# PEER gather of expert rows: two of each eight dot products moved from VectorE to GpSimd and ScalarE, h read from PSUM

## The chip, the cores and the metric

The kernel runs on one core of a Trainium2 chip, in float32. The metric is the device time of one execution in microseconds (us), from the first to the last instruction.

## The reference, cut to what matters

256 tokens of width 2048 go through a gated-MLP layer, an attention layer and a mixer with convolution and mLSTM; the last part is a layer of product-key experts (PEER). The change touches only that one. For each token 8 heads pick 16 of 16384 experts, so 128 picks a token:

```
ue  = take(u, eid)                                  # 128 rows of 2048 floats for each token
act = gelu(einsum('thkd,td->thk', ue, xt))          # one dot product of 2048 for each pick
ve  = take(v, eid)
out = einsum('thk,thkd->td', gate * act, ve)
```

What the change rearranges is the einsum in the second line: 256 tokens times 128 picks, each a dot of a gathered row of `u` with the token's row of h.

## The kernel before, in words

The tokens are two tiles of 128, one token in each partition. A pick of a tile is then one gather: an indirect DMA that GpSimd issues (L560) brings 128 rows of 8 KB, one to each partition, 1 MB in all. There are 256 of them, 128 in each tile. They land in `ring`, eight slots of SBUF; slot s holds pick s of a batch of eight.

VectorE does three things in this stage (L1887 to L1903):

- `choose(n)` finds the experts of a group n (2 heads, 32 picks, four batches) with maxima, index searches and one-hot look-ups. Eight groups, four to a tile; the choice of group n+1 stands ahead of the dots of group n, so no choice stands between groups 6 and 7.
- `dot_rows(n)` (L1838) waits for each slot to land (`gathered`, L1823) and does one fused multiply and sum over 2048 elements (L1847), both operands in SBUF: `ring[:, s, :]` and `h[:, t, :]`. After eight of them it copies the eight dots to `wgt` (L1856) and stages the indices of the batch after the next (`stage`, L1817).
- In tile 1 it also builds, once a batch, the one-hot matrices of eight tokens of tile 0 (`one_hots`, L1827). TensorE multiplies them (`scatter`, L917), and ScalarE stores the products as `wT` (`store_w`, L1209).

GpSimd runs a loop of 16 gathers (L549). It waits for `idx_ready` at the start of a batch, and before each gather for `rows_used`, the count of dots done, so that the slot it overwrites is free. Between the gathers it has no other work.

ScalarE does the exponentials of the gates (L1192), the gelu of a tile's dots (L1198), the copies of transposed picks (L1204) and the stores of `wT`.

At the end of a tile `weights(t)` (L1859) waits for the gelu, multiplies by the gates and waits until TensorE has transposed the weights and ScalarE has copied them out of PSUM (units `wgtT0`, `wgtT1`; the keys go the same way earlier, as `pkT0`, `pkT1`). Then the one-hots of tile 1 follow alone, and after them the product with the dense three quarters of `v` and the gathered last quarter.

PSUM is two halves of 2048 floats a partition, A and B, handed from unit to unit in the order of the list `UNITS` (L83). In this stage half A takes `scores1` and then both halves take the small units of the picks; the scatter alternates between A and B.

Of the kernel before, what the change touches and what calls it, by code (L numbers as in the profile page):

```python
# [71 lines left out]
SCATTER = 8  # L72
# [70 lines left out]
def build(nc, x, norm_g, a_w_in, a_v_norm_g, a_w_s, a_b_s, a_w_out, b_w_in, b_w_out, final_g, ln_in_g_2, ln_in_b_2,  # L143
# [6 lines left out]
    with ctx:  # L150
# [180 lines left out]
        def sem(name):  # L331
            return ctx.enter_context(nc.semaphore(name))
# [161 lines left out]
        def _(pool):  # L494
# [54 lines left out]
            with pool.Fori(0, TILES * PICKS // BODY) as i:  # L549
                for n in range(BODY):  # L550
                    b, s = divmod(n, GATHER_SLOTS)
                    if s == 0:
                        pool.wait_ge(idx_ready[b], i + 1)
                    if s == GATHER_SLOTS // 2:

                        pool.wait_ge(products, CHUNKS)

                    pool.wait_ge(rows_used, i * BODY + (n + 1))
                    pool.nop(nofuse=True)
                    nc.gpsimd.indirect_dma_start(  # L560
                        out=ring[:, s, :], out_offset=None, in_=peer_u_2[0],
                        in_offset=bass.IndirectOffsetOnAxis(ap=idx[:, b, s:s + 1], axis=0),
                    ).then_inc(row_landed[s], 16)
# [22 lines left out]
        def _(pe):  # L586
# [322 lines left out]
            def turn_picks(unit, srcs):  # L909

                is_free(pe, unit)
                hf = halves(unit)
                for n, src in enumerate(srcs):
                    last = nc.tensor.transpose(ps[hf][:, 3, n * P:(n + 1) * P], src, ident[:, :])  # L914
                filled_by(last, unit)

            def scatter(t):  # L917

                with pe.Fori(0, P // SCATTER // 2) as i:
                    for s in range(2):  # L920
                        m = i * 2 + (t * (P // SCATTER) + s)
                        pe.wait_ge(onehot_done, m + 1)
                        pe.wait_ge(w_stored, m + 1)
                        for n in range(SCATTER):
                            last = mm(by_128[s][:, n, :], onehot_b[:, s, n, :], onehot_a[:, s, n, :], start=True, stop=True)  # L925
                        last.then_inc(scattered, 1)

            pe.sem_inc(scattered, 2)
            emptied("peer_q1")()
            for t in range(TILES):  # L930
                pe.wait_ge(keys_known, t + 1)
                turn_picks(f"pkT{t}", [pick_keys[:, t, half, :] for half in range(2)])
                pe.wait_ge(wgt_done, t + 1)
                turn_picks(f"wgtT{t}", [wgt[:, t * PICKS:(t + 1) * PICKS]])
                scatter(t)

            def multiply_v(c, s, first=False, last=False):
# [31 lines left out]
        def _(act):  # L969
# [221 lines left out]
            scores_out(1)()  # L1191
            def gate_exponent(n):  # L1192
                t, q = divmod(n, TILE_GROUPS)
                act.wait_ge(gate_sub, n + 1)
                cut = gate[:, t, q * GROUP_HEADS:(q + 1) * GROUP_HEADS, :]
                fn(cut, cut, ACT.Exp).then_inc(gate_exp, 1)  # L1196

            def pick_gelu(t):  # L1198

                act.wait_ge(idx_ready[1], (t + 1) * PICKS // (2 * GATHER_SLOTS) + 1)  # L1200
                cut = wgt[:, t * PICKS:(t + 1) * PICKS]
                fn(cut, cut, ACT.Gelu).then_inc(gelu_done, 1)

# [5 lines left out]
            def store_w(t, first, count):  # L1209

                with act.Fori(0, count // 2) as i:
                    for s in range(2):
                        m = i * 2 + (first + s)
                        act.wait_ge(scattered, m + (t * (P // SCATTER) + 3))
                        fn(wT[:, 1 - t, :, bass.ds(m * SCATTER, SCATTER)],  # L1215
                           by_128[s][:, 0:SCATTER, :].rearrange("p n a -> p a n"), ACT.Copy).then_inc(w_stored, 1)
# [49 lines left out]
        def _(dve):  # L1266
# [571 lines left out]
            def dot_rows(n, batches=0):  # L1838

                t, q = divmod(n, TILE_GROUPS)  # L1840
                first = n * GROUP_PICKS
                per = batches // (GROUP_PICKS // BODY)
                with dve.Fori(0, GROUP_PICKS // BODY) as i:
                    for b in range(2):
                        for s in range(GATHER_SLOTS):
                            gathered(i, first + b * GATHER_SLOTS, s)
                            v.tensor_tensor_reduce(out=ring[:, s, :], in0=ring[:, s, :], in1=h[:, t, :], scale=1.0,  # L1847
                                                   scalar=0.0, op0=ALU.mult, op1=ALU.add,
                                                   accum_out=dots[:, b, s:s + 1]).then_inc(rows_used, 1)
                            done = b * GATHER_SLOTS + s + 1  # L1850
                            if done * per % BODY == BODY // 2:
                                m = q * batches + done * per // BODY
                                one_hots(m % 2, i * per + m, i * (per * SCATTER) + m * SCATTER)

                        dve.wait_ge(rows_used, i * BODY + (first + (b + 2) * GATHER_SLOTS))
                        v.tensor_copy(wgt[:, bass.ds(i * BODY + (first + b * GATHER_SLOTS), GATHER_SLOTS)], dots[:, b, :])  # L1856
                        stage(b, i * BODY + (first + (b + 2) * GATHER_SLOTS))

            def weights(t):  # L1859

                dve.wait_ge(gelu_done, t + 1)
# [4 lines left out]
                is_emptied(dve, f"wgtT{t}")  # L1866

            dve.sem_inc(rows_used, GATHER_SLOTS)
# [125 lines left out]
```

## Time and profile before

| | us |
|---|---|
| median of 3 runs (3248.04 to 3255.05) | 3249.94 |
| span of the profiled execution | 3249.8 |
| first gather to last dot (1815.8 to 2576.0 in the span) | 760 |
| VectorE busy / ScalarE / GpSimd / TensorE, whole span | 2225 / 1095 / 825 / 2417 |
| granted TensorE clock, mean of the span | 0.872 |

All times are positions in the span of the profiled execution or durations in it. The stage of the change lies between 1815 and 2576 us. Before it the stream of dense weights runs; after it the one-hots of tile 1 (to 2632) and the product with `v` (to the end).

### The profile page before, as it was taken

Reading aid. Unit: us, or ns where it says so; the run is one execution under the profiler, and the core shown is the slowest. Engines: PE = TensorE matmul, PEld = TensorE weight load, DVE = VectorE, ACT = ScalarE, POOL = GpSimd, SP = SyncE. Lnnn points to the kernel's source line nnn. Section 1 sums busy time; section 2 is a strip of 40 time slices with the busy share of each in tenths; the row PEclk is TensorE's granted clock in tenths of the full one; section 3 lists DMA queues with packets and bytes.
Section 4 is the critical chain, followed back from the end, with each engine's and each line's share of the span. In section 5 each row is a group of like instructions: output and inputs, shape, how many; then the busy total and the mean of one; then the engine's idle time right before and its main releaser. Section 6 shows DMA issues by size and latency. Waiting matters only on the chain.

```text
span 3249.8 us, 32810 instructions
## 1 busy us (share of the span) xinstructions
PE 2416.7 (74%) x10945; PEld 1994.8 (61%) x10945; DVE 2225.1 (68%) x2822; ACT 1095.1 (34%) x1069; POOL 824.5 (25%) x548
## 2 busy tenths in 40 slices
PE   7999999999999998999998400001111389998996
PEld 6888888888888886888887400001111267777775
DVE  4456455555445556356656899999999987777777
ACT  4444444444445543344444100000000134343343
POOL 1000000000000000000000466676557435555553
PEclk8999999999999998899999755555555699999998
DMA  7666556556665454455564688898789548888886
GB/s 246 194 187 185 178 181 188 186 190 188 185 184 162 136 201 157 143 162 182 181 231 140 267 368 363 373 410 339 308 315 381 230 166 287 284 285 296 282 284 211
DMA packets 164690, 766.49 MB, mean 236 GB/s; under 512 B 20124, under 2 KB 20176, under 8 KB 130672
## 3 DMA queue, kind: packets, MB, share of 16 engines
q1 hardware_dynamic: 104800, 415.28, 39.9%
q0 software_dynamic: 59792, 349.90, 27.7%
q8 instruction: 62, 1.02, 0.1%
q14 instruction: 36, 0.29, 0.0%
HBM read 763.00 MB, written 2.10 MB: 235 GB/s over the span
## 4 chain that ended last, share of the span: by engine, by line
PE 54%; DVE 25%; DMA 11%; issue 6%; ACT 3%; DVEq 1%; SPq 0%; POOL 0%; POOLq 0%; ACTq 0%
PE half L600 49%; DVE ring L1847 14%; DMA v_raw<-in_peer_v 9%; DVE v_split L1928 3%; ACT v_split L1229 2%; DVE onehot_a L1834 2%; PE half L619 1%; DMA v_rows<-in_peer_v,idx 1%; DMA w_raw<-in_a_w_in 1%; DVE onehot_b L1830 1%; PE half L941 1%; PE half L796 1%; DVEq L1834 0%; PE half L668 0%; DVE left L1745 0%
## 5 line engine op out<-in xcount | busy, mean ns | idle before, releaser
L600 PE MATMUL half<-w_split,xT 128*128 128x512 f32 x7104 | 1639.4, 392 | 14.8 <-DVE xT L1296 12.2
L600 PEld LDWEIGHTS half<-w_split,xT 128*128 128x128 f32 x7104 | 1338.1, 189 | 294.4 <-issue 8.1
L1277 DVE TENSOR_TENSOR w_split<-w_raw,w_split 128x1024 fp32r<-128x1024 f32 x592 | 722.5, 1225 | 764.6 <-ACT w_split L981 763.8
L981 ACT ACTIVATE w_split<-w_raw 128x1024 fp32r<-128x1024 f32 x592 | 626.5, 1059 | 943.2 <-PE half L600 914.8
L560 POOL DMA_INDIRECT ring<-in_peer_u,idx x256 | 480.9, 1878 | 439.6 <-DVE dots L1847 186.2
L941 PE MATMUL half<-v_split,w_x 128*128 128x512 f32 x2304 | 548.6, 395 | 46.0 <-ACT v_split L1229 43.3
L1847 DVE CUSTOM_DVE_ANT_0 ring<-ring,h 128x2048 f32<-128x2048 f32 x256 | 570.0, 2285 | 5.0 <-issue 2.5
L941 PEld LDWEIGHTS half<-v_split,w_x 128*128 128x128 f32 x2304 | 428.6, 189 | 165.8 <-ACT v_split L1229 76.0
L574 POOL DMA_INDIRECT v_rows<-in_peer_v,idx x256 | 327.9, 1281 | 333.6 <-DVE v_odd L1911 209.2
L925 PE MATMUL half<-onehot_a,onehot_b 128*128 128x128 f32 x512 | 95.0, 362 | 334.8 <-DVE onehot_a L1834 334.8
L925 PEld LDWEIGHTS half<-onehot_a,onehot_b 128*128 128x128 f32 x512 | 87.9, 268 | 342.1 <-DVE onehot_a L1834 342.1
L1928 DVE TENSOR_TENSOR v_split<-v_raw,v_split 128x1536 fp32r<-128x1536 f32 x128 | 225.0, 1758 | 102.4 <-ACT v_split L1229 102.3
L1229 ACT ACTIVATE v_split<-v_raw 128x1536 fp32r<-128x1536 f32 x128 | 190.6, 1489 | 292.5 <-DMA v_raw<-in_peer_v 292.5
L498 POOL DMA_DIRECT2D row_a<-in_final_g x1 | 0.5, 531 | 1130.2 <-DVE ao L1503 1130.2
L1215 ACT ACTIVATE wT<-half 128x1024 f32 x32 | 32.8, 1024 | 395.6 <-PE half L925 395.6
L914 PE MATMUL half<-ident,wgt 128*128 128x128 f32 x2 | 0.9, 473 | 186.2 <-DVE wgt L1863 186.2
L914 PE MATMUL half<-ident,pick_keys 128*128 128x128 f32 x4 | 1.0, 353 | 184.1 <-DVE v_odd L1877 184.1
L1911 DVE SCALAR_TENSOR_TENSOR v_odd<-v_rows,wgt,v_odd 128x512 f32<-128x512 f32 x128 | 95.8, 748 | 36.2 <-DMA v_rows<-in_peer_v,idx 35.8
L914 PEld LDWEIGHTS half<-ident,wgt 128*128 128x128 f32 x2 | 0.4, 180 | 186.8 <-DVE wgt L1863 186.8
L914 PEld LDWEIGHTS half<-ident,pick_keys 128*128 128x128 f32 x4 | 0.6, 177 | 184.3 <-issue 184.3
L1911 DVE SCALAR_TENSOR_TENSOR h<-v_rows,wgt,h 128x512 f32<-128x512 f32 x128 | 95.4, 745 | 7.1 <-DMA v_rows<-in_peer_v,idx 7.1
L1196 ACT ACTIVATE gate<-gate 128x32 f32<-128x32 f32 x8 | 1.7, 225 | 264.6 <-DVE gate L1778 264.6
(287 smaller groups left out, 1201.2 us busy)
## 6 DMA issues: line engine op xcount, KB each, us to landing
w_raw<-in_a_w_in SPq DMA_DIRECT2D x192, 512.0 KB, 3.6
v_raw<-in_peer_v SPq DMA_DIRECT2D x128, 768.0 KB, 5.8
w_raw<-in_b_w_in SPq DMA_DIRECT2D x128, 512.0 KB, 3.5
w_raw<-in_w_in SPq DMA_DIRECT2D x112, 512.0 KB, 3.5
w_raw<-in_a_w_out SPq DMA_DIRECT2D x64, 512.0 KB, 3.6
w_raw<-in_b_w_out SPq DMA_DIRECT2D x32, 512.0 KB, 4.6
w_raw<-in_w_out SPq DMA_DIRECT2D x32, 512.0 KB, 4.6
w_raw<-in_peer_wq SPq DMA_DIRECT2D x32, 512.0 KB, 3.7
```

Of the source, the lines that this page charges most:

```text
L560: nc.gpsimd.indirect_dma_start(out=ring[:, s, :], out_offset=None, in_=peer_u_2[0], in_offset=bass.IndirectOffsetOnAxis(ap=idx[:, b, s:s + ...
L574: nc.gpsimd.indirect_dma_start(out=v_rows[n % V_SLOTS][:, :], out_offset=None, in_=peer_v_2[0].rearrange("e (s d) -> (e s) d", s=V_PARTS), ...
L600: last = mm(ps[half][:, 2 * t + n, :], xt[:, xp, kk, tok], w_split[:, s, wp, n * BANK:(n + 1) * BANK], start=(k == 0 and xp == 0 and wp == ...
L925: last = mm(by_128[s][:, n, :], onehot_b[:, s, n, :], onehot_a[:, s, n, :], start=True, stop=True)
L941: ins = mm(ps[t][:, n, :], w_x[s][:, xp, 1 - t, 0, :], v_split[s][:, vp, n * BANK:(n + 1) * BANK], start=first and xp + vp == 0, stop=last ...
L981: fn(w_split[:, k % SPLIT_SLOTS, 0, :], w_raw[:, k % RAW_SLOTS, :], ACT.Copy).then_inc(hi_done, 1)
L1229: fn(v_split[s][:, 0, :], v_raw[s][:, :], ACT.Copy).then_inc(v_hi, 1)
L1277: v.tensor_tensor(w_split[:, s, 1, :], w_raw[:, k % RAW_SLOTS, :], w_split[:, s, 0, :].bitcast(F32), ALU.subtract).then_inc(split_done, 1)
L1834: ins = v.tensor_scalar(onehot_a[:, s, n, :], iota_keys[:, :], picksT[:, 0, bass.ds(token + n, 1)], picksT[:, 2, bass.ds(token + n, 1)], A ...
L1847: v.tensor_tensor_reduce(out=ring[:, s, :], in0=ring[:, s, :], in1=h[:, t, :], scale=1.0, scalar=0.0, op0=ALU.mult, op1=ALU.add, accum_out ...
L1911: v.scalar_tensor_tensor(out=acc, in0=v_rows[m % V_SLOTS][:, :], scalar=wgt[:, bass.ds(i * BODY + m, 1)], in1=acc, op0=ALU.mult, op1=ALU.a ...
L1928: v.tensor_tensor(v_split[s][:, 1, :], v_raw[s][:, :], v_split[s][:, 0, :].bitcast(F32), ALU.subtract)\
```

## The change

The dots of slots 2 and 6 of each batch (`POOL_ROWS`) leave VectorE. GpSimd multiplies the landed row by h in place, and ScalarE sums the product with an accumulating copy. VectorE does the other six, and reads h from PSUM: ScalarE copies h of tile 0 into half B and of tile 1 into half A before the first dot, and these halves are held for it through their tile, so the picks' units become `picks0` in B and `picks1` in A, with keys and weights transposed together after the weights are done, and the scatter of tile 0 uses half B alone.

GpSimd's order is written out by hand: product of slot 2, gathers of slots 0, 1, 2 for the next batch, product of slot 6, gathers of 3, 4, 5, 7, 6. The gather of a slot waits for `rows_used` (a VectorE dot) or, for 2 and 6, for `rows_summed` (a ScalarE sum). At the end of each batch VectorE waits for `rows_summed` of both rows before it copies the dots.

```diff
+POOL_ROWS = (2, 6)
+DVE_ROWS = tuple(s for s in range(GATHER_SLOTS) if s not in POOL_ROWS)
...
-       ("pkT0", A, False), ("wgtT0", A, False), ("pkT1", A, False), ("wgtT1", A, False)]
+       ("picks0", B, False), ("picks1", A, False)]
...
+            def regather(j, b, s):
+                if s in POOL_ROWS:
+                    pool.wait_ge(rows_summed, j * len(POOL_ROWS) + (POOL_ROWS.index(s) + 1))
+                else:
+                    pool.wait_ge(rows_used, j * len(DVE_ROWS) + (DVE_ROWS.index(s) + 1))
+                gather_u(b, s)
+
+            def scale_row(t, j, s):
+                pool.wait_ge(row_landed[s], j * 16 + 16)
+                nc.gpsimd.tensor_tensor(ring[:, s, :], ring[:, s, :], h[:, t, :], ALU.mult).then_inc(rows_scaled, 1)
+
+            def scale_and_gather(t, i, b, last=False):
+                j = i * 2 + (t * BATCHES + b)
+                scale_row(t, j, POOL_ROWS[0])
+                if not last:
+                    pool.wait_ge(idx_ready[1 - b], i + (t * BATCHES // 2 + 1 + b))
+                    for s in (0, 1, 2):
+                        regather(j, 1 - b, s)
+                scale_row(t, j, POOL_ROWS[1])
+                if not last:
+                    for s in (3, 4, 5, 7, 6):
+                        regather(j, 1 - b, s)
...
-                            last = mm(by_128[s][:, n, :], onehot_b[:, s, n, :], onehot_a[:, s, n, :], start=True, stop=True)
+                            last = mm(by_128[B][:, s * SCATTER + n, :], onehot_b[:, s, n, :], onehot_a[:, s, n, :],
+                                      start=True, stop=True)
...
-                turn_picks(f"pkT{t}", [pick_keys[:, t, half, :] for half in range(2)])
                 pe.wait_ge(wgt_done, t + 1)
-                turn_picks(f"wgtT{t}", [wgt[:, t * PICKS:(t + 1) * PICKS]])
+                turn_picks(f"picks{t}", [pick_keys[:, t, half, :] for half in range(2)]
+                           + [wgt[:, t * PICKS:(t + 1) * PICKS]])
+                emptied(f"picks{t}")()
...
+            is_emptied(act, "peer_q1")
+            fn(flat[B], h[:, 0, :], ACT.Copy).then_inc(h_copied, 1)
             scores_out(1)()
+            is_emptied(act, "scores1")
+            fn(flat[A], h[:, 1, :], ACT.Copy).then_inc(h_copied, 1)
+
+            def sum_rows(n, i, b, store=False):
+                for k, s in enumerate(POOL_ROWS):
+                    j = i * 2 + (n * GROUP_PICKS // GATHER_SLOTS + b)
+                    act.wait_ge(rows_scaled, j * len(POOL_ROWS) + (k + 1))
+                    fn(ring[:, s, :], ring[:, s, :], ACT.Copy, accum_out=dots[:, b, s:s + 1]).then_inc(rows_summed, 1)
...
+            def sum_and_store_group(n, first):
+                with act.Fori(0, GROUP_PICKS // (2 * GATHER_SLOTS)) as i:
+                    for b in range(2):
+                        sum_rows(n, i, b)
+                        store_one(0, i * 2 + (first + b), b)
...
-                        for s in range(GATHER_SLOTS):
+                        for s in DVE_ROWS:
                             gathered(i, first + b * GATHER_SLOTS, s)
-                            v.tensor_tensor_reduce(out=ring[:, s, :], in0=ring[:, s, :], in1=h[:, t, :], scale=1.0,
+                            v.tensor_tensor_reduce(out=ring[:, s, :], in0=ring[:, s, :], in1=flat[1 - t], scale=1.0,
...
-                        dve.wait_ge(rows_used, i * BODY + (first + (b + 2) * GATHER_SLOTS))
-                        v.tensor_copy(wgt[:, bass.ds(i * BODY + (first + b * GATHER_SLOTS), GATHER_SLOTS)], dots[:, b, :])
+                        for s in POOL_ROWS:
+                            gathered(i, first + b * GATHER_SLOTS, s)
                         stage(b, i * BODY + (first + (b + 2) * GATHER_SLOTS))
+                        dve.wait_ge(rows_used, j * len(DVE_ROWS) + len(DVE_ROWS))
+                        dve.wait_ge(rows_summed, j * len(POOL_ROWS) + len(POOL_ROWS))
+                        v.tensor_copy(wgt[:, bass.ds(i * BODY + (first + b * GATHER_SLOTS), GATHER_SLOTS)], dots[:, b, :])\
+                            .then_inc(dots_taken, 1)
...
+                if n == 0:
+                    dve.wait_ge(h_copied, TILES)
```

## Rows read from the trace of the kernel before

**Rows 1.** The page: the span in 40 slices of 81 us, then the chain.

```profile
DVE  4456455555445556356656899999999987777777
...
POOL 1000000000000000000000466676557435555553
...
PE 54%; DVE 25%; DMA 11%; issue 6%; ACT 3%; DVEq 1%; SPq 0%; POOL 0%; POOLq 0%; ACTq 0%
```

**Rows 2.** Groups by line, 1780 to 2680 us: busy us, mean ns, idle before.

```profile
L1847 DVE CUSTOM_DVE_ANT_0 ring<-ring,h 128x2048 f32<-128x2048 f32 x256 | 570.0, 2285 | 5.0 <-issue 2.5 <-DVE gate L1815 1.8 <-ACT picksT L1003 0.7
L560 POOL DMA_INDIRECT ring<-in_peer_u,idx x256 | 480.9, 1878 | 439.6 <-DVE dots L1847 186.2 <-DVE idx L1819 178.8 <-issue 74.6
```

**Rows 3.** First dot of groups 0, 4, 5, 6, and the copy after group 7's last.

```profile
1834.88 2.29 DVE L1847 CUSTOM_DVE_ANT_0 ring<-ring,h 128x2048 f32<-128x2048 f32 x1 [0.27 <-DVE gate L1815]
...
2196.40 2.29 DVE L1847 CUSTOM_DVE_ANT_0 ring<-ring,h 128x2048 f32<-128x2048 f32 x1 [0.69 <-ACT picksT L1003]
...
2299.10 2.29 DVE L1847 CUSTOM_DVE_ANT_0 ring<-ring,h 128x2048 f32<-128x2048 f32 x1 [0.26 <-DVE gate L1815]
...
2403.53 2.29 DVE L1847 CUSTOM_DVE_ANT_0 ring<-ring,h 128x2048 f32<-128x2048 f32 x1 [0.26 <-DVE gate L1815]
...
2576.10 0.17 DVE L1856 COPY wgt<-dots 128x8 f32 x1 [0.15 <-DVE dots L1847]
```

**Rows 4.** Windows: us, busy PE, PEld, DVE, ACT, POOL, clock, DMA share, GB/s.

```profile
1880.00:1890.00 10.00, 0.00 (x0) 0.00 (x0) 9.87 (x13) 0.00 (x0) 8.78 (x5) 0.50 1.02 423
1890.00:1900.00 10.00, 0.00 (x0) 0.00 (x0) 10.00 (x9) 0.00 (x0) 8.48 (x6) 0.50 1.01 420
1920.00:1930.00 10.00, 0.00 (x0) 0.00 (x0) 9.40 (x16) 0.00 (x0) 2.14 (x1) 0.50 0.16 65
```

**Rows 5.** Instructions in order: gathers before the first dot and among dots.

```profile
1818.36 0.94 POOL L560 DMA_INDIRECT ring<-in_peer_u,idx  x1 [0.30 <-issue]
...
1839.32 2.29 DVE L1847 CUSTOM_DVE_ANT_0 ring<-ring,h 128x2048 f32<-128x2048 f32 x1
1840.50 1.91 POOL L560 DMA_INDIRECT ring<-in_peer_u,idx  x1 [0.31 <-issue]
...
1841.53 2.29 DVE L1847 CUSTOM_DVE_ANT_0 ring<-ring,h 128x2048 f32<-128x2048 f32 x1
```

**Rows 6.** Groups by line and shape, whole span: operands in PSUM (half), and sums.

```profile
L1706 DVE TENSOR_TENSOR cz<-half,cz 128x2048 f32<-128x2048 f32 x1 | 2.3, 2282 | 0.0
...
L1035 ACT ACTIVATE x_trash<-h 128x2048 f32<-128x2048 f32 x2 | 3.8, 1906 | 0.0
...
L1035 ACT ACTIVATION_READ_ACCUMULATOR q_trash<-h 128x1 f32 x4 | 0.7, 186 | 0.0
```

**Rows 7.** Groups by line and shape, whole span: GpSimd's elementwise work.

```profile
L508 POOL MEMSET ones<- 128x256 f32 x1 | 0.3, 312 | 0.1
L505 POOL TENSOR_SCALAR_AFFINE_SELECT upto<-upto 128x128 f32<-128x128 f32 x1 | 0.3, 294 | 0.1
...
L504 POOL MEMSET onward<- 128x128 f32 x1 | 0.2, 205 | 0.1
```

**Rows 8.** Line L560: all gathers of u, from issue to landing.

```profile
DMA to landing us min/median/max: 5.5/9.5/15.6
```

**Rows 9.** Instructions in order: end of group 0's dots, choice, first dot of group 1.

```profile
1907.71 0.17 DVE L1856 COPY wgt<-dots 128x8 f32 x1 [0.15 <-DVE dots L1847]
...
1913.45 0.69 DVE L1772 TENSOR_TENSOR cand<-sv 128x512 f32<-128x512 f32 x1
...
1924.78 2.29 DVE L1847 CUSTOM_DVE_ANT_0 ring<-ring,h 128x2048 f32<-128x2048 f32 x1 [0.26 <-DVE gate L1815]
```

**Rows 10.** Instructions in order: the one-hots inside a batch of tile 1.

```profile
2205.25 1.22 DVE L1830 TENSOR_TENSOR onehot_b<-iota_keys,picksT 128x1024 f32<-128x1024 f32 x1
2206.39 2.13 DVE L1834 TENSOR_SCALAR onehot_a<-iota_keys,picksT 128x128 f32<-128x128 f32 x8
2208.44 2.28 DVE L1847 CUSTOM_DVE_ANT_0 ring<-ring,h 128x2048 f32<-128x2048 f32 x1
```

**Rows 11.** Instructions in order: start of the stage, and the hand-over between the tiles.

```profile
1830.49 1.88 ACT L1003 ACTIVATE scores_b<-half 128x2048 f32<-128x2048 f32 x1 [6.92 <-PE half L899]
...
1834.01 0.18 DVE L1813 TENSOR_REDUCE gsum<-gate 128x2 f32<-128x32 f32 x1 [3.27 <-ACT gate L1196]
...
2195.81 0.28 ACT L1003 ACTIVATE picksT<-half 128x128 f32<-128x128 f32 x1 [16.81 <-PE half L914]
```

More of the change, by code:

```diff
@@ L384, in build @@
         rows_used = sem("rows_used")
+        h_copied = sem("h_copied")
+        rows_scaled = sem("rows_scaled")
+        rows_summed = sem("rows_summed")
+        dots_taken = sem("dots_taken")
         gelu_done = sem("gelu_done")
@@ L548, in _ @@
             BODY = 2 * GATHER_SLOTS
[L549 to L563, printed above, removed]
+            BATCHES = PICKS // GATHER_SLOTS
@@ new lines, in gather_u @@
+            def gather_u(b, s):
+                pool.nop(nofuse=True)
+                nc.gpsimd.indirect_dma_start(
+                    out=ring[:, s, :], out_offset=None, in_=peer_u_2[0],
+                    in_offset=bass.IndirectOffsetOnAxis(ap=idx[:, b, s:s + 1], axis=0),
+                ).then_inc(row_landed[s], 16)
+            def regather(j, b, s):
[4 more added lines that the diff above has]
+                gather_u(b, s)
@@ new lines, in _ @@
+            pool.wait_ge(idx_ready[0], 1)
+            for s in range(GATHER_SLOTS):
+                if s == GATHER_SLOTS // 2:
+                    pool.wait_ge(products, CHUNKS)
+                gather_u(0, s)
+            with pool.Fori(0, BATCHES // 2) as i:
+                for b in range(2):
+                    scale_and_gather(0, i, b)
+            with pool.Fori(0, BATCHES // 2 - 1) as i:
+                for b in range(2):
+                    scale_and_gather(1, i, b)
+            scale_and_gather(1, BATCHES // 2 - 1, 0)
@@ L565, in _ @@
+            scale_and_gather(1, BATCHES // 2 - 1, 1, last=True)
             for t in range(TILES):
@@ L1190, in _, with sum_group @@
             turned("pqT1", pqT[:, 8:16, :])()
+            is_emptied(act, "peer_q1")
+            fn(flat[B], h[:, 0, :], ACT.Copy).then_inc(h_copied, 1)
             scores_out(1)()
+            is_emptied(act, "scores1")
[5 more added lines that the diff above has]
+                    fn(ring[:, s, :], ring[:, s, :], ACT.Copy, accum_out=dots[:, b, s:s + 1]).then_inc(rows_summed, 1)
+            def sum_group(n):
+                with act.Fori(0, GROUP_PICKS // (2 * GATHER_SLOTS)) as i:
+                    for b in range(2):
+                        sum_rows(n, i, b)
+            def sum_and_store_group(n, first):
+                with act.Fori(0, GROUP_PICKS // (2 * GATHER_SLOTS)) as i:
+                    for b in range(2):
+                        sum_rows(n, i, b)
+                        store_one(0, i * 2 + (first + b), b)
             def gate_exponent(n):
@@ L1198, in pick_gelu @@
             def pick_gelu(t):
-                act.wait_ge(idx_ready[1], (t + 1) * PICKS // (2 * GATHER_SLOTS) + 1)
+                act.wait_ge(dots_taken, (t + 1) * PICKS // GATHER_SLOTS)
                 cut = wgt[:, t * PICKS:(t + 1) * PICKS]
@@ L1207, in picks_out, with store_one, store_w @@
                 take(unit, dst, ps[hf][:, 3, 0:count * P].rearrange("p (k t) -> p k t", t=P))
-            def store_w(t, first, count):
-                with act.Fori(0, count // 2) as i:
+            def store_one(t, m, s):
+                act.wait_ge(scattered, m + (t * (P // SCATTER) + 3))
+                fn(wT[:, 1 - t, :, bass.ds(m * SCATTER, SCATTER)],
+                   by_128[B][:, s * SCATTER:(s + 1) * SCATTER, :].rearrange("p n a -> p a n"), ACT.Copy)\
+                    .then_inc(w_stored, 1)
+            def store_w(t):
+                with act.Fori(0, P // SCATTER // 2) as i:
                     for s in range(2):
[L1213 to L1216, printed above, removed]
+                        store_one(t, i * 2 + s, s)
             act.sem_inc(w_stored, 2)
@@ L1229, in round_v @@
                 fn(v_split[s][:, 0, :], v_raw[s][:, :], ACT.Copy).then_inc(v_hi, 1)
-            for n in range(TILE_GROUPS + 1):
-                gate_exponent(n)
+            gate_exponent(0)
+            for n in range(TILE_GROUPS):
+                gate_exponent(n + 1)
+                sum_group(n)
             pick_gelu(0)
-            picks_out("pkT0", picksT[:, 0:2, 0:P], 2)
-            picks_out("wgtT0", picksT[:, 2:3, 0:P], 1)
+            picks_out("picks0", picksT[:, :, 0:P], 3)
             share = P // SCATTER // TILE_GROUPS
             for q in range(TILE_GROUPS):
-                store_w(0, q * share, share)
                 if q + 1 < TILE_GROUPS:
                     gate_exponent(TILE_GROUPS + q + 1)
-            picks_out("pkT1", picksT[:, 0:2, P:], 2)
+                sum_and_store_group(TILE_GROUPS + q, q * share)
             warm_up(ACT.Gelu)
             pick_gelu(1)
-            picks_out("wgtT1", picksT[:, 2:3, P:], 1)
+            picks_out("picks1", picksT[:, :, P:], 3)
             round_v(0, 0)
-            store_w(1, 0, P // SCATTER)
+            store_w(1)
             act.wait_ge(w_stored, TOKENS // SCATTER + 2)
@@ L1844, in dot_rows @@
                     for b in range(2):
-                        for s in range(GATHER_SLOTS):
+                        j = i * 2 + (first // GATHER_SLOTS + b)
+                        for s in DVE_ROWS:
                             gathered(i, first + b * GATHER_SLOTS, s)
-                            v.tensor_tensor_reduce(out=ring[:, s, :], in0=ring[:, s, :], in1=h[:, t, :], scale=1.0,
+                            v.tensor_tensor_reduce(out=ring[:, s, :], in0=ring[:, s, :], in1=flat[1 - t], scale=1.0,
                                                    scalar=0.0, op0=ALU.mult, op1=ALU.add,
@@ L1865, in weights @@
                 step(v.tensor_scalar(h[:, t, V_DENSE:], h[:, t, V_DENSE:], ALPHA, None, ALU.mult))
[L1866 to L1868 removed]
+                is_emptied(dve, f"picks{t}")
             dve.sem_inc(v_used, V_SLOTS)
```

1 line of the change is left out of this document (removed).

## The prediction

> **What bounds the kernel now.** I read the page first: its slices show VectorE at nine tenths from 1790 to 2600 us while GpSimd stands at four to seven, and the chain gives VectorE a quarter of the span [rows 1]. The groups by line then say that in the gather the 256 dots take 570 us and stood idle for 5.0 us in all [rows 2]: no dot ever waited for a row. So VectorE bounds this stage, with a pace of 2.21 us a dot [rows 5]. The periods follow [rows 3]: tile 0 takes 361.5 us (1834.88 to 2196.40), four groups of 90.4; tile 1 takes 102.7, 104.4 and, for groups 6 and 7 with no choice between them, 172.6 us (2403.53 to 2576.10).
>
> The view that decides is another one. Among the dots the DMA engines are fully busy and move 420 to 423 GB/s [rows 4]. A gather is 128 x 8 KB = 1.05 MB, so a row costs the DMA engines 2.48 us and a batch of eight 19.8 us; VectorE asks for one every 18.2. The queue falls behind during four batches and catches up in the choice, whose end shows 65 GB/s [rows 4]. A group of tile 0 needs 32 x 2.48 = 79.3 us of transfer in its 90. **VectorE is bound by a hair; the DMA engines are the next wall**, and freeing VectorE of a quarter of the dots cannot bring a batch under 19.8 us. A ring of eight slots also holds only one batch ahead.
>
> **The parts and their prices.** The whole sum is made against the profiled span of 3249.8 us, which is the median of 3249.94 to within 0.2 us.
>
> *Dot from PSUM.* A VectorE product with one operand in PSUM and 2048 elements took 2282 ns, the dot from SBUF 2285 [rows 2, 6]. I price the dot at 2.21 us as before; six are 13.3 us.
>
> *Gather.* Alone it took 0.94 us with a gap of 0.30 [rows 5]: 1.24. Among the dots it took 1.91, because it ends 0.88 us after the running dot ends (1839.32 + 2.21 = 1841.53; 1840.50 + 1.91 = 1842.41). I take it that GpSimd waits there for a dot that reads two operands from SBUF, and that a dot with one from PSUM frees it: 1.24 us. Bounds: 1.24 and 2.21.
>
> *Product on GpSimd.* No row shows a two-input operation there. A memset costs 205 ns for 128 elements and 312 for 256: 0.84 ns an element, on a base of 98 ns; a one-input select of 128 costs 294, so the read adds 0.69 ns an element [rows 7]. A write alone over 2048 is 1.8 us, the lower bound; two one-input passes (98 + 2048 x 1.53 = 3.2 each) are 6.5, the upper. One write and two reads are 98 + 2048 x 2.22 = 4.6 us, which I take, 4.7 with its gap. The Trainium skill's "GPSIMD Engine Reference", section "Elementwise — side-by-side cycle accounting", gives 4497 ns for this shape; by it the sum would be some 4 us lower.
>
> *Sum on ScalarE.* 1906 + 186 ns [rows 6]: 2.1 us, on an engine idle in this stage.
>
> *GpSimd's batch.* 2 x 4.7 + 8 x 1.24 = 19.3 us. GpSimd had waited for VectorE; it now stands as near the wall as the DMA engines.
>
> *The loop.* Slot 6 is gathered last and multiplied late. Let it land at L. Product to L+4.7; gather of slot 3 at L+4.9, landing 5.5 later with an empty queue [rows 8], and 4, 5, 7, 6 behind it at 2.48 each: L' = L + 4.9 + 5.5 + 9.9 = **L + 20.3**. In between GpSimd has its other five gathers' and product's work (done at L+19.4). So a batch costs 20.3 us. VectorE is no limit, but it waits at each batch's end for the sum of slot 6, which comes at L + 4.7 + 2.1 + 0.3 = L + 7.1.
>
> *A group of tile 0, from its first dot.* Dots of the landed batch end at 2.2, 4.4, 6.6, 8.8, 11.1 and 13.3. Gathers of 0, 1, 2 end by 7.1 (product 2 was made during the choice), product 6 by 11.8, its sum by 14.2. Gather 3 starts at 11.9, so L of the second batch is 11.9 + 5.5 + 9.9 = 27.3, then 47.6 and 67.9; VectorE goes on at 67.9 + 7.1 = 75.0. The choice follows, 17.1 us [rows 9]: 92.1 against 90.0 in the first period (1834.88 to 1924.78) [rows 3, 9]. What was saved in the dots is spent at the group's end, where **VectorE stands still for the last row's transfer, product and sum** before it may choose.
>
> *The choice beside a product.* GpSimd ends its gathers at 78.8 and multiplies slot 2 until 83.6. The choice's first two-input operation comes 5.7 us into it [rows 9], at 80.7. If what held a gather back behind a dot works the other way too, it waits 2.9 us: 95.0, or +5.1 on a period. The Trainium skill, "SBUF — State Buffer", section "SBUF: two separate sides", says just this: VectorE and GpSimd share a pair of ports, an exclusive lock for a whole instruction, taken by VectorE when it has two SBUF inputs. The gathers above agree with it (0.94 against 1.91); no run here shows the other direction. By it the forecast holds; without it, the first rival. Tile 0: 4 x 5.1 = **+20.6**.
>
> *Tile 1.* One-hots add 3.2 us to a batch of VectorE [rows 10], after slot 3. In the loop VectorE has room (13.3 + 3.2 in 20.3). With the lock, product 6 (started about 7.9) holds the second part of the first batch's one-hots until 12.6; dots 4, 5, 7 end at 17, 19, 21, the gathers wait for them, GpSimd's batch ends at 23.8 instead of 18.0, the next batches cost 20.7 because gathers and one-hots meet, and the group's dots take 81.6. With the choice (17.1 + 2.9): 101.6 and, with the index work after group 5's, 102.9, against 102.7 and 104.4: -2.6. Groups 6 and 7: 81.6 + 1.2 + 4 x 20.7 = 165.6 against 172.6: -7.0. Sum **-9.6**.
>
> *Ends.* The first dot waits for h in PSUM: the copy of tile 0 fits into ScalarE's wait of 6.92 us, that of tile 1 follows `scores_b` and precedes the gates' exponentials, for which VectorE waited already [rows 11]: **+1.9**. At both tiles' ends keys and weights turn together: two more transposes and a copy of 384 instead of 128 columns behind the 0.28 us one [rows 11]: **+1.0** in all. The scatter on one half: the store is 1.0 us and TensorE is mostly idle, zero. ScalarE's order (two sums, then a store) delays nothing, as the store's scatter lies in the same batch.
>
> Sum: 20.6 - 9.6 + 1.9 + 1.0 = +13.9: **3264 us**. A measurement of this kernel can tell 0.2% (6.5 us) from no change.
>
> **The rivals.**
>
> 1. *GpSimd's products don't hold VectorE's short operations.* Tile 0: 4 x 2.1 = +8.4. Tile 1: 92.1 and 93.1 for 102.7 and 104.4, and 75.0 + 1.2 + 81.2 = 157.4 for 172.6: -37. With the ends: -25, **3225**. For it: VectorE's dots kept 2.21 us while gathers ran beside them. Against: those gathers read only one index a partition. Its place is the choice and the one-hots; it decides at stalls under some 1.5 us a group. Chance 0.24.
> 2. *Stalls only in part*, the two tiles cancel: 3244 to 3256. Chance 0.13.
> 3. *The product is cheap*, 3.5 us or less. The loop then sits on 19.8 us and the group's end comes 3 us earlier or more; 1.8 us would give 3177, 3.5 about 3210. Against it stands the price of a read in [rows 7]. Chance 0.08.
> 4. *The product is dear*, near 6.5 us. GpSimd alone sets 23.3 us a batch, a group of tile 0 about 106: +64 there, +15 in tile 1: 3330. Chance 0.08.
> 5. *The change doesn't do what it says*: a dot from PSUM still holds GpSimd back. Gathers keep 2.21 us, products wait for a dot's end: 8 x 2.21 + 2 x 5.8 = 29.3 us a batch, 9 or more over the 20.3 in 32 batches: about 3550. Nothing here runs GpSimd beside a PSUM operand. Chance 0.05.
>
> **How the numbers follow.** The forecast has 0.42 and its own range of 3250 to 3285 (product 4.4 to 5.0 us, stall 2 to 4 us). Rivals 1 and 3 are faster: 0.32. Same: rival 2 and a slice of the forecast, 0.16. Slower: 0.39 + 0.08 + 0.05 = 0.52. The range runs from 3215 (rival 1 with a product a little cheaper) to 3305 (a product of 5.5 us, half way to rival 4), leaving out the cheapest products, the dearest ones and rival 5.
>
> **What would show it.** In the changed profile: dots near 2285 ns; gathers near 0.94 us in GpSimd's row; a tensor_tensor row of about 4.6 us, 64 of them; batches of 20 to 21 us; VectorE's copy of the dots waiting for ScalarE's sums, some 6 us a batch; in the choice an idle gap of about 3 us ahead of L1772's counterpart; DMA still near 420 GB/s in the groups. Wrong if periods of tile 0 come out under 90 us: then the product is cheaper, or the landing after GpSimd's pause is quicker than the 5.5 us that I gave it.

## The result and the profile after

The changed kernel takes 3302.88 us (median of 4 runs, 3301.86 to 3306.76) against 3248.99 in the same runs for the kernel before: ratio 1.0165, 95% interval 1.0149 to 1.018. It is slower, as forecast, but by 54 us where 14 were forecast. The span of the profiled execution is 3302.0 us, 52.2 more than before.

The page of the changed kernel, slices of 82.6 us and the chain, answers to [rows 1]:

```profile
DVE  4456454555445556357566888888998887777777
...
POOL 1000000000000000000000766676657525555454
...
DMA  6665555556665454446643988897789638788886
...
PE 52%; DVE 15%; DMA 12%; issue 11%; POOL 5%; ACT 3%; DVEq 1%; SPq 0%; POOLq 0%; ACTq 0%
```

VectorE has dropped from nine tenths to eight, and its share of the chain from 25% to 15%; GpSimd, which was 0% of the chain, now holds 5%.

The groups by line, 1780 to 2680 us (busy us, mean ns, idle before), answer to [rows 2]. L1917 is the dot, L559 the gather, L575 the product, L1242 the sum:

```profile
L1917 DVE CUSTOM_DVE_ANT_0 ring<-ring,half 128x2048 f32<-128x2048 f32 x192 | 431.7, 2283 | 32.4 <-DMA ring<-in_peer_u,idx 26.7 <-issue 2.1 <-DVE gate L1884 1.8
L575 POOL TENSOR_TENSOR ring<-ring,h 128x2048 f32<-128x2048 f32 x64 | 289.8, 4528 | 76.5 <-DMA ring<-in_peer_u,idx 72.5 <-DVE dots L1917 3.2
L559 POOL DMA_INDIRECT ring<-in_peer_u,idx x256 | 252.6, 987 | 367.1 <-DVE idx L1888 178.1 <-DVE dots L1917 128.5 <-issue 53.5
L1242 ACT ACTIVATE ring<-ring 128x2048 f32<-128x2048 f32 x64 | 122.2, 1909 | 546.5 <-POOL ring L575 546.5
...
L1888 DVE COPY idx<-eid 128x8 uint32 x32 | 76.5, 2391 | 4.5 <-DMA ring<-in_peer_u,idx 4.5
...
L1840 DVE CAST sif<-si 128x64 f32<-128x64 uint32 x8 | 19.0, 2374 | 0.2
...
L1930 DVE COPY wgt<-dots 128x8 f32 x32 | 5.8, 180 | 54.9 <-ACT ring L1242 54.4 <-issue 0.5
```

Every price of a part was right: dot 2283 ns, gather down from 1878 to 987 (most are 0.94), product 4528, sum 1909 + 186. And 138 us of dots left VectorE. They came back as waiting, 32.4 us before dots, mostly for rows in flight, and 54.9 before the copy of the dots, and in instructions that are stretched: the copy of eight indices from 171 to 2391 ns, the cast from 193 to 2374. The stretched copy of the indices stands between VectorE's last dot and its copy of the dots, so it is part of the same wait for the last sum. GpSimd stood idle for 72.5 us ahead of products, waiting for a row to land.

The first dot of groups 0, 1, 4, 5, 6 and the copy after the last dot, answering to [rows 3]:

```profile
1834.52 2.29 DVE L1917 CUSTOM_DVE_ANT_0 ring<-ring,half 128x2048 f32<-128x2048 f32 x1 [0.26 <-DVE gate L1884]
...
1935.62 2.29 DVE L1917 CUSTOM_DVE_ANT_0 ring<-ring,half 128x2048 f32<-128x2048 f32 x1 [0.26 <-DVE gate L1884]
...
2240.17 2.29 DVE L1917 CUSTOM_DVE_ANT_0 ring<-ring,half 128x2048 f32<-128x2048 f32 x1 [1.50 <-ACT picksT L1043]
...
2344.80 2.29 DVE L1917 CUSTOM_DVE_ANT_0 ring<-ring,half 128x2048 f32<-128x2048 f32 x1 [0.26 <-DVE gate L1884]
...
2450.11 2.29 DVE L1917 CUSTOM_DVE_ANT_0 ring<-ring,half 128x2048 f32<-128x2048 f32 x1 [0.26 <-DVE gate L1884]
...
2624.80 0.21 DVE L1930 COPY wgt<-dots 128x8 f32 x1 [2.14 <-ACT ring L1242]
```

| | before | forecast | after |
|---|---|---|---|
| tile 0, four groups | 361.5 | 382 | 405.7 |
| group 4, group 5 | 102.7, 104.4 | 101.6, 102.9 | 104.6, 105.3 |
| groups 6 and 7 | 172.6 | 165.6 | 174.7 |

The excess over the forecast is 24 us in tile 0, about 6 in each group, and 14 in tile 1: 3.0 and 2.4 in groups 4 and 5 and 9.1 in groups 6 and 7. One batch in the middle of group 1 shows it, from one product 6 to the next (the wait in brackets stood before the instruction):

```profile
1964.66 4.50 POOL L575 TENSOR_TENSOR ring<-ring,h 128x2048 f32<-128x2048 f32 x1 [2.61 <-DMA ring<-in_peer_u,idx]
1964.79 4.38 DVE L1888 COPY idx<-eid 128x8 uint32 x1 [0.37 <-DMA ring<-in_peer_u,idx]
...
1969.30 0.97 POOL L559 DMA_INDIRECT ring<-in_peer_u,idx  x1
...
1971.33 0.18 DVE L1930 COPY wgt<-dots 128x8 f32 x1 [2.15 <-ACT ring L1242]
...
1976.82 2.29 DVE L1917 CUSTOM_DVE_ANT_0 ring<-ring,half 128x2048 f32<-128x2048 f32 x1 [0.55 <-DMA ring<-in_peer_u,idx]
...
1987.13 4.50 POOL L575 TENSOR_TENSOR ring<-ring,h 128x2048 f32<-128x2048 f32 x1 [3.47 <-DMA ring<-in_peer_u,idx]
```

The batch takes 22.5 us, not 20.3. Product 6 runs 4.5 us; VectorE gets no further from 1964.4 to 1971.3 (4.4 us in the stretched copy of the indices, then idle), the 7 us that were forecast. Gather 3 is issued at 1969.30 and its row is multiplied at 1976.82, when it lands: 7.5 us, not 5.5. Slots 4, 5, 7 and 6 follow 2.5 to 2.8 us apart, and GpSimd stands 3.47 us before it can multiply slot 6. Windows of the same stretch (us, PE, PEld, DVE, ACT, POOL, clock, DMA share, GB/s):

```profile
1966.60:1968.60 2.00, 0.00 (x0) 0.00 (x0) 2.00 (x1) 0.00 (x0) 2.00 (x1) 0.50 1.04 438
...
1970.60:1972.60 2.00, 0.00 (x0) 0.00 (x0) 1.00 (x2) 0.59 (x2) 1.69 (x2) 0.50 0.76 238
1972.60:1974.60 2.00, 0.00 (x0) 0.00 (x0) 2.00 (x3) 0.00 (x0) 1.39 (x3) 0.50 1.01 344
1974.60:1976.60 2.00, 0.00 (x0) 0.00 (x0) 1.68 (x2) 0.00 (x0) 1.98 (x2) 0.50 0.96 348
...
1980.60:1982.60 2.00, 0.00 (x0) 0.00 (x0) 1.80 (x3) 1.23 (x2) 1.27 (x2) 0.50 1.01 426
```

The queue falls to 238 GB/s after the product's pause and needs 8 us to be back at 426: the batch of 22.5 us is 2.7 us longer than the 19.8 that its transfer needs at full pace. In the choice (after group 0) the product holds VectorE's cast, while the search before it keeps its 0.28 us:

```profile
1919.69 4.50 POOL L575 TENSOR_TENSOR ring<-ring,h 128x2048 f32<-128x2048 f32 x1
...
1920.05 0.28 DVE L1822 FIND_INDEX8 si<-sv,left 128x8 uint32<-128x128 f32 x1
...
1921.15 3.10 DVE L1840 CAST sif<-si 128x64 f32<-128x64 uint32 x1
1924.29 0.69 DVE L1841 TENSOR_TENSOR cand<-sv 128x512 f32<-128x512 f32 x1
```

The cast ends with the product, 2.9 us late.

### The profile page after: what moved, and what is told of

The parts are those of the page before. It is cut to its first block, busy times and chain, and to the rows that moved or that the text cites. A ratio compares the mean times of both kernels' runs of the same rounds, so it can differ in the third digit from the quotient of the medians.

```text
span 3302.0 us, 33040 instructions
## 1 busy us (share of the span) xinstructions
PE 2412.7 (73%) x10945; PEld 1993.3 (60%) x10945; DVE 2194.2 (66%) x2694; ACT 1225.5 (37%) x1197; POOL 883.5 (27%) x612
## 4 chain that ended last, share of the span: by engine, by line
PE 52%; DVE 15%; DMA 12%; issue 11%; POOL 5%; ACT 3%; DVEq 1%; SPq 0%; POOLq 0%; ACTq 0%
PE half L639 48%; DMA v_raw<-in_peer_v 9%; POOL ring L575 3%; DVE v_split L2003 3%; DVE ring L1917 3%; ACT v_split L1298 2%; POOL ring L559 2%; DVE onehot_a L1903 2%; DMA v_rows<-in_peer_v,idx 1%; PE half L658 1%; DMA ring<-in_peer_u,idx 1%; DMA w_raw<-in_a_w_in 1%; DVE sif L1840 1%; DVE onehot_b L1899 1%; PE half L835 0%
## 5 line engine op out<-in xcount | busy, mean ns | idle before, releaser
L1917 DVE CUSTOM_DVE_ANT_0 ring<-ring,half 128x2048 f32<-128x2048 f32 x192 | 431.7, 2283 | 32.4 <-DMA ring<-in_peer_u,idx 26.7
L559 POOL DMA_INDIRECT ring<-in_peer_u,idx x256 | 252.6, 987 | 367.1 <-DVE idx L1888 178.1
L1242 ACT ACTIVATE ring<-ring 128x2048 f32<-128x2048 f32 x64 | 122.2, 1909 | 546.5 <-POOL ring L575 546.5
L575 POOL TENSOR_TENSOR ring<-ring,h 128x2048 f32<-128x2048 f32 x64 | 289.8, 4528 | 76.5 <-DMA ring<-in_peer_u,idx 72.5
L1888 DVE COPY idx<-eid 128x8 uint32 (+1 forms) x66 | 82.2, 1247 | 4.5 <-DMA ring<-in_peer_u,idx 4.5
```

The lines of the kernel that those rows point to most:

```text
L559: nc.gpsimd.indirect_dma_start(out=ring[:, s, :], out_offset=None, in_=peer_u_2[0], in_offset=bass.IndirectOffsetOnAxis(ap=idx[:, b, s:s + ...
L575: nc.gpsimd.tensor_tensor(ring[:, s, :], ring[:, s, :], h[:, t, :], ALU.mult).then_inc(rows_scaled, 1)
```

## The experiments

The theory: the change is slow by where GpSimd's products stand (a queue that runs dry, a wait at a group's end, a stall in the choice), and reading h from PSUM costs nothing. The rivals: the move to PSUM or the hand-over to ScalarE costs by itself; GpSimd's total decides, wherever its products stand. In the kernels below GpSimd's batch is written as a list, shown here in short: `pS` multiplies slot S of this batch, `gS` gathers slot S of the next. e3 to e10 change this list and `POOL_ROWS` alone, but for e7, which is e4 with one operand changed; in e1 ScalarE's sums and VectorE's wait for them go with the products. Each was timed beside the kernel before, whose medians were 3251.32 (e1 to e4), 3250.91 (e5 to e8) and 3251.03 (e9, e10).

### e1: h in PSUM alone

```diff
-POOL_ROWS = (2, 6)
-ORDER = "p2 g0 g1 g2 p6 g3 g4 g5 g7 g6"
+POOL_ROWS = ()
+ORDER = "g0 g1 g2 g3 g4 g5 g6 g7"
```

> All eight dots of a batch are VectorE's, with h in PSUM; no product on GpSimd, no sum on ScalarE. Theory (the cost of the change lies in where GpSimd's products stand, the move to PSUM is free): dots keep 2.21 us, gathers fall from 1.91 to 0.94 us, but VectorE still asks for a batch every 18.2 us against 19.8 us of transfer, so periods of tile 0 stay at 90 us and the time at 3249, within 5 us of the kernel before. Rival (the dot from PSUM or the order of the picks costs something by itself): 3260 or more.

3250.66 us, ratio 0.9993 (0.9983 to 1.0003). The first period of tile 0 is 89.3 us. The move to PSUM, and the picks turned together, cost and bring nothing by themselves that this interval (5.5 us less to 1 us more) would show.

### e2: the products left out

```diff
-                nc.gpsimd.tensor_tensor(ring[:, s, :], ring[:, s, :], h[:, t, :], ALU.mult).then_inc(rows_scaled, 1)
+                pool.sem_inc(rows_scaled, 1)
```

> The changed kernel with the two products on GpSimd left out (ScalarE sums the rows unmultiplied, so two of eight dots of each batch are not dots); every wait, gather and sum stays in its place. Theory: with no pause of 4.5 us between gathers the queue never runs dry, batches fall from 22.5 to 19.8-20 us, the wait at a group's end from 7.1 to 2.6 us, the stall in the choice from 2.9 us to nothing: periods of tile 0 near 85 us instead of 101, time about 3171. Rival (the hand-over to ScalarE and its semaphores cost, not the products): periods stay above 95, time above 3260.

3186.0 us, ratio 0.9798 (0.9781 to 0.9814). Periods of tile 0 are 85.3 to 87.8 us, batches at most 19.9, the transfer's own pace. With every wait, gather and sum in place, 117 us of the changed kernel's time hang on the two products. This doesn't tell yet whether on their total or on their places; it came 15 us above what I had expected.

### e3: two products, early slots

```diff
-POOL_ROWS = (2, 6)
-ORDER = "p2 g0 g1 g2 p6 g3 g4 g5 g7 g6"
+POOL_ROWS = (0, 4)
+ORDER = "p0 g1 g0 g2 g3 p4 g5 g4 g6 g7"
```

> Still two products a batch, but of slots 0 and 4 instead of 2 and 6, and the order product 0, gathers 1, 0, 2, 3, product 4, gathers 5, 4, 6, 7, so that the last row to land is one of VectorE's. Theory: batches of about 20.5 us (GpSimd's own 19 us and the transfer's 19.8), a group's end 2.3 us after its last landing instead of 7.1: periods of tile 0 near 88 us, time about 3204 (3185 to 3230). Rival (what costs is GpSimd's total of two products and eight gathers, wherever they stand): 3290 to 3305.

3300.59 us, ratio 1.0154 (1.0137 to 1.0171): here my expectation failed and the rival's number came out. Its order of time says why (lines of a batch in group 1; L560 is the gather, L576 the product):

```profile
1964.27 4.50 POOL L576 TENSOR_TENSOR ring<-ring,h 128x2048 f32<-128x2048 f32 x1
1965.07 3.74 DVE L1890 COPY idx<-eid 128x8 uint32 x1
...
1968.93 0.97 POOL L560 DMA_INDIRECT ring<-in_peer_u,idx  x1 [0.16 <-issue]
1970.94 0.17 DVE L1932 COPY wgt<-dots 128x8 f32 x1 [2.13 <-ACT ring L1244]
...
1971.57 0.94 POOL L560 DMA_INDIRECT ring<-in_peer_u,idx  x1 [1.68 <-ACT ring L1244]
...
1975.02 4.53 POOL L576 TENSOR_TENSOR ring<-ring,h 128x2048 f32<-128x2048 f32 x1
...
1985.80 4.51 POOL L576 TENSOR_TENSOR ring<-ring,h 128x2048 f32<-128x2048 f32 x1
```

A batch takes 21.5 us, in which GpSimd has no idle time except 1.68 us twice, before the gather of the slot it has just multiplied: I had put that gather one place behind the product, and ScalarE's sum takes longer than one gather. GpSimd is the wall, its second product of a batch starts only as VectorE's last dot ends, and VectorE waits for that sum again.

### e5: the same with the gather of a multiplied slot later

```diff
-ORDER = "p0 g1 g0 g2 g3 p4 g5 g4 g6 g7"
+ORDER = "p0 g1 g2 g0 g3 p4 g5 g6 g4 g7"
```

> As e3, with the gather of a multiplied slot two gathers later (product 0, gathers 1, 2, 0, 3, product 4, gathers 5, 6, 4, 7), so that ScalarE's sum is done when GpSimd comes to it. In e3 GpSimd never idled but for 2 x 1.68 us of that wait in each 21.5 us. Theory (GpSimd was the wall in e3, by its order): batches fall to 19.8-20 us, GpSimd's 19.0 and the transfer's 19.8, and once GpSimd keeps up, the group's end follows VectorE's last dot: time 3200 to 3230. Rival (with 19.0 of 19.8 us GpSimd stays behind, each product comes a batch late and VectorE waits for its sum at a group's end): batches of 20 us but groups still near 96 us, time 3255 to 3275.

3239.01 us, ratio 0.996 (0.9947 to 0.9974). Batches in tile 0 are 19.1 us, periods 92. It lies between the two expectations. Swapping two neighbours in each half of the list brought 62 us against e3, with the same products, gathers and sums, so their total doesn't decide; but VectorE still waits 56.6 us in all for sums ahead of the copy of the dots, as the rival had it.

### e6: the changed kernel with two gathers ahead of product 6

```diff
-ORDER = "p2 g0 g1 g2 p6 g3 g4 g5 g7 g6"
+ORDER = "p2 g0 g1 g2 g3 g4 p6 g5 g7 g6"
```

> The changed kernel with one thing moved: gathers 3 and 4 stand ahead of product 6, so five rows are queued while GpSimd multiplies, not three. Theory (the changed kernel's 22.5 us a batch are a queue that runs dry in that pause): batches of 20 us as the prediction had them, periods of tile 0 near 95 us, time 3255 to 3268. Rival (VectorE's wait for the sum of slot 6 sets the loop: 4.5 + 2.1 + 13.3 us of dots and the gathers behind them): batches of 21.5 to 22.5 us, time 3285 to 3302.

3258.68 us, ratio 1.0027 (1.0017 to 1.0037): within the theory's range. The same 69 us in both kernels, first of e6:

```profile
1936.00:2005.00 69.00, 0.00 (x0) 0.00 (x0) 60.16 (x55) 14.02 (x14) 59.09 (x36) 0.50 1.00 412
```

then of the changed kernel:

```profile
1936.00:2005.00 69.00, 0.00 (x0) 0.00 (x0) 58.76 (x51) 12.02 (x12) 51.76 (x32) 0.50 0.89 349
```

The same kernel with two gathers in another place fills the DMA engines to 1.00 and 412 GB/s instead of 0.89 and 349. The first period of tile 0 is 93.0 us, 75.5 to the last copy of the dots (81.2 in the changed kernel) and 17.5 of choice (19.9).

So the move did two things. With two gathers fewer behind product 6, the next product 2 starts 1.6 us into the choice, not 3.9, and is nearly over when VectorE comes to its cast; line of e6:

```profile
1917.49 0.76 DVE L1842 CAST sif<-si 128x64 f32<-128x64 uint32 x1
```

The six casts that took 3.10 us take 0.76: 14 us. **Of the 54 us that the change costs, e6 takes back 44: 14 are the stall in the choice, and about 30 are the batches, whose queue no longer runs dry behind product 6.** What is left, 8 us (5.5 in the profiled executions), is 12 us more in tile 0, 9 less in tile 1 and 2 more ahead of the first dot; VectorE's waits for the last sum, 67.2 us in all ahead of the copy of the dots, stand against the dots that it no longer does, and no run separates the two.

### e4, e8 and e9: one product a batch

```diff
-POOL_ROWS = (2, 6)
-ORDER = "p2 g0 g1 g2 p6 g3 g4 g5 g7 g6"
+POOL_ROWS = (0,)
+ORDER = "p0 g1 g0 g2 g3 g4 g5 g6 g7"
```

That is e4. The order of e8 is `p0 g1 g2 g0 g3 g4 g5 g6 g7`, that of e9 `p0 g0 g1 g2 g3 g4 g5 g6 g7`.

> One product a batch, slot 0, in the order product 0, gathers 1, 0, 2 to 7; VectorE does seven dots. Theory: transfer-bound, 19.8-20 us a batch in both tiles (VectorE's own 15.5, with one-hots 18.8), group's end 2.3 us after the last landing, some 2 us of stall in the choice: periods of tile 0 near 86, of tile 1 near 88, time about 3181. Rival (GpSimd's total): half way between e1 and the changed kernel, about 3275.

> e4 with the gather of slot 0 one place later, behind ScalarE's sum. Theory: GpSimd loses its wait of up to 1.7 us, but it was not the wall with one product: 3205 to 3212, the same as e4. Rival (GpSimd's time decides with one product too): 3190 or less.

> e4 with slot 0 gathered first, before slot 1: product 0 of the next batch then starts about 1.5 us into the choice, where it started 2.3 us (e4) and 4.8 us (e8) into it. Theory (a product that is running when the choice reaches its first copy of indices holds VectorE for its rest; 1.65 us in e4, 4.12 in e8): the cast takes under 0.9 us, periods of tile 0 near 87 us, and the time is 3 to 8 us under e4: 3202 to 3208. Rival (e8's loss came from its order of gathers, not from the stall; GpSimd here waits 2 us more in each batch): 3210 to 3225.

| | time | ratio (95%) | product starts, after the choice | cast | period of group 1 |
|---|---|---|---|---|---|
| e4 | 3209.93 | 0.9871 (0.9855 to 0.9888) | 2.5 us | 1.65 us | 88.2 us |
| e8 | 3220.26 | 0.9903 (0.9887 to 0.992) | 5.0 us | 4.12 us | 90.9 us |
| e9 | 3215.32 | 0.9888 (0.9871 to 0.9904) | 1.5 us | 0.67 us | 89.0 us |

e4 beats both kernels, by 41 us against the one before: the row of slot 0 lands early, its product and sum are done long before the batch ends, and VectorE has 15.5 us of dots, 18.8 with one-hots, and waits 4.4 us in all ahead of the copy of the dots, not 54.9. Its gain is 36 us in tile 1, where VectorE was the wall with 21.4 us a batch (343.6 for 379.7 us), and 7 in tile 0, where the transfer is. It came 29 us short of my expectation, mostly since the groups with a choice in tile 1 take 94.0 and 95.2 us and not 88, and those of tile 0 88 to 91, not 86.

e8 was expected to equal e4 and is 10 us slower. Its row lands later, so the product starts later in the choice and holds the cast for its rest, 2.5 us longer in four of the choices, which is the 10 us; the dots of its groups take as long as e4's. Lines of e8:

```profile
2000.90 4.49 POOL L576 TENSOR_TENSOR ring<-ring,h 128x2048 f32<-128x2048 f32 x1 [3.50 <-DMA ring<-in_peer_u,idx]
2001.32 4.12 DVE L1842 CAST sif<-si 128x64 f32<-128x64 uint32 x1
```

e9 put it the other way: the cast fell to 0.67 us as expected, but the time didn't fall with it. GpSimd waits there for each sum before the next gather (127.2 us in all, 31.9 in e4), the dots of a group take 1.7 us more, and the stall that was saved is paid there. That is the rival's range.

### e7: one product, h in SBUF

```diff
-                            v.tensor_tensor_reduce(out=ring[:, s, :], in0=ring[:, s, :], in1=flat[1 - t], scale=1.0,
+                            v.tensor_tensor_reduce(out=ring[:, s, :], in0=ring[:, s, :], in1=h[:, t, :], scale=1.0,
```

> e4 with VectorE's dots reading h from SBUF again, as before the change. Theory (a dot with two operands in SBUF and a product on GpSimd exclude each other, and gathers wait for the dot's end): gathers back at 1.9 us, products and dots one after the other, batches of 22 to 25 us, time above 3290. Rival (they don't, and the copy of h to PSUM was for nothing): 3210, as e4.

3335.7 us, ratio 1.0261 (1.0241 to 1.0282). e4 without the PSUM operand is 126 us slower. Lines of one batch:

```profile
1960.22 5.75 POOL L576 TENSOR_TENSOR ring<-ring,h 128x2048 f32<-128x2048 f32 x1
1961.54 6.58 DVE L1919 CUSTOM_DVE_ANT_0 ring<-ring,h 128x2048 f32<-128x2048 f32 x1
...
1969.26 1.88 POOL L560 DMA_INDIRECT ring<-in_peer_u,idx  x1 [0.30 <-issue]
```

The product waits for the running dot's end (5.75 for 4.5 us), the next dot for the product's (6.58 for 2.29), and gathers are back at 1.9. So h in PSUM brings nothing alone (e1) and is what makes a product on GpSimd pay.

### e10: the product clear of the choice

```diff
-POOL_ROWS = (0,)
-ORDER = "p0 g1 g0 g2 g3 g4 g5 g6 g7"
+POOL_ROWS = (2,)
+ORDER = "g0 g1 p2 g3 g4 g2 g5 g6 g7"
```

> One product a batch, of slot 2, behind gathers 0 and 1, in the order gathers 0, 1, product 2, gathers 3, 4, 2, 5, 6, 7. GpSimd then stands before gather 0 while VectorE chooses, so no product meets the choice. Theory: the cast is back at 0.2 us, but in each group's first batch the gathers of slots 2 to 7 start 4.5 us later (tile 0: +2 us a period against e4), and in tile 1 the product meets the one-hots, which wait 2 us or more a batch: 3225 to 3250. Rival (the stall in the choice is what matters, the rest is slack): 3200 or less.

3273.52 us, ratio 1.0071 (1.0054 to 1.0087). The cast is back at 195 ns, tile 0 has periods of 89.3 to 89.9 in its first three groups, and tile 1 loses more than I allowed, so that both expectations were missed: its batches take 23.1 us (19.1 in e4), as the one-hots of a batch meet the product.

```profile
2221.31 4.51 POOL L576 TENSOR_TENSOR ring<-ring,h 128x2048 f32<-128x2048 f32 x1
2221.71 5.20 DVE L1901 TENSOR_TENSOR onehot_b<-iota_keys,picksT 128x1024 f32<-128x1024 f32 x1
```

An operation of 1.22 us takes 5.20 here and 3.30 in the mean. A product has to be kept from the work of VectorE that it holds in every stage, not only in one.

## Why the prediction was right or wrong

The direction was right and the size was not: 54 us for 14. The measured time lies in the stated range only by luck, for its upper end of 3305 us stood for a product of 5.5 us, which didn't come; the forecast's own range of 3250 to 3285 was missed.

*What bounds.* Right: VectorE by a hair, then the transfer. e2 shows the second wall: batches of up to 19.9 us for the 19.8 worked out.

*Prices.* Right: the dot (2283 ns), the gather (0.94 us), the product (4.6 taken, 4.53 measured), the sum. Rivals 3 and 4, a cheap or a dear product, and rival 5, a dot from PSUM that holds GpSimd back, are out by these rows; e7 shows rival 5's waits, with the operand in SBUF.

*The loop.* **This step failed**, the term "L' = L + 20.3". It took a gather issued after the pause to land in 5.5 us and the DMA engines to be at full pace from then on. Measured: the batch takes 22.5, gather 3 lands after 7.5 us. The three batches behind a group's first make 6.2 us (21.6, 22.8 and 22.7 in group 0, for 20.2, 20.3 and 20.3), and the last copy of group 0's dots stood at 1915.75, 81.2 us after its first dot, for the 75.0 of the forecast. Times four in tile 0 that makes up the 24 us of excess there; in tile 1 it is again the later batches, and the two tiles make 38 of the 39 us. e6 removes the pause's effect by order alone: the same stretch takes 75.5, 74.8, 74.9 and 75.4 us in its four groups of tile 0, which is the forecast's 75.0. (Its time of 3259 is below the forecast's 3264 because its casts wait less as well.) The term did have the pause in it, but at too low a price: slot 3 was to land at L + 10.4, only 0.5 us behind a queue without a gap (four rows of 2.48), and it landed 2.3 us behind it (1976.8, where L is 1964.6). The mechanism was right and this size was off.

*The group's end.* Right: VectorE waits for the last row's landing, product and sum; the 7 us are there, and with the loop above they are why a quarter less work on VectorE brought nothing in tile 0. e5 and e6 still carry this wait (56.6 and 67.2 us); e4, whose multiplied row lands early, does not (4.4).

*The choice beside a product.* Right and nearly exact: 2.9 us were worked out, the cast took 3.10 instead of 0.19, and the choice with the gates took 19.9 us (1915.75 to 1935.62) for the 20.0 of the forecast. The Trainium skill's "SBUF — State Buffer", section "SBUF: two separate sides", which I had set behind this step, is borne out in both directions by e7 (a product of 5.75 us behind a dot, a dot of 6.58 behind a product). Rival 1 is out, and e8 against e4 shows that such a stall costs time: 10 us. The first operation to be held was the cast, one place ahead of the two-operand one that I named; it has one input, so the case of two SBUF inputs that I had gone by doesn't cover it. That the 2.9 us came out all the same is the nearness of the two.

*Tile 1.* Half right. The one-hots of a group's first batch are stretched (6.31 us for 2.13 in group 4) and the gathers wait for the dots behind them, as forecast: the second batch ended 39.5 us into the group, for 40.2 in the forecast (81.6 less two batches of 20.7). It was again the later ones that were long, 22.5 and 22.8 for 20.7.

*Ends.* The start cost nothing (-0.4 us for +1.9), and from the last copy of the dots to the first one-hot of tile 1 it takes 4.7 us, not 2.2: 2.5 us for the 0.5 allowed. ScalarE's store of `wT` and its load of the gelu table now come behind the last sum.

## What to carry to other kernels

When an engine that issues gathers is also given work, count what is queued behind each pause: product + landing time must be less than the queued rows' transfer, or the order of the issues has to be changed before anything else is judged. In this kernel five rows queued (12.4 us) were enough in most batches for a product of 4.5 and a landing of 5.5 us, three (7.4 us) were not. Give the slower pair of engines the rows that land first, so that their result is not the last thing a batch waits for. Moving one of eight dots paid (0.987 at best, but 1.007 with a product that meets the one-hots), two of eight hardly (1.017 as written, 0.996 at best here): with two, GpSimd's 19 us a batch stood as near the wall as the transfer's 19.8 and any wait on it was on the path.

## What the runs showed of the hardware

A gather issued into a queue that is running out lands late, and by more than the landing time of an empty queue explains. Landings of the gather of slot 3 in the changed kernel, issued at 1947.80 and at 1969.30:

```profile
DMA to landing us min/median/max: 5.4/5.4/5.4
...
DMA to landing us min/median/max: 7.5/7.5/7.5
```

Both were issued 2.7 us before the landing of the row ahead of them; the first landed 2.6 us after that row, the second 4.8, and the row behind each came 4.0 and 2.8 us later. So the two rows after a pause are the better measure, 5.0 us at full pace. In the groups of tile 0, for every gather that comes straight behind a product:

| still queued at the issue | two rows take | seen |
|---|---|---|
| 5.0 to 7.8 us, e6 and changed kernel | 4.9 to 5.0 us | 33 times |
| 3.6 to 4.5 us, e6 | 5.1 to 7.1 us | 7 times |
| 2.2 to 2.8 us, changed kernel | 6.6 to 8.0 us | 16 times |

The first column is the time from the issue to the landing of the row ahead. The forecast's reckoning (a landing of 5.5 us after an issue 2.7 us ahead, then full pace) would have made the last row 5.3 us. Why a queue that is nearly out loses more than that, no run here shows.

A product on GpSimd holds VectorE's copy of eight indices (0.17 to 4.39 us), the cast (0.19 to 4.13), one-hots of either kind (1.22 to 5.20 and 2.13 to 6.31) and dots from SBUF (2.29 to 6.58) for its rest. It doesn't hold searches (0.28 us beside a product as without one), maxima or dots with an operand in PSUM (2.29).
